# Output product of a hybrid attention layer: attention and hyena halves as three products of rounded parts, and the hyena half two to a step

## The chip, the cores and the metric

The kernel runs on one core of a Trainium2 chip. The metric is device time in microseconds (us) of one execution, as the median of several runs. Engines: PE (TensorE, the matrix engine), DVE (VectorE), ACT (ScalarE), POOL (GpSimd) and SP (SyncE, which issues most DMAs).

## The reference, cut to what matters

One layer over 640 tokens (512 latent, 128 context), five tiles of 128. After a common input projection, attention and a hyena long convolution run side by side. Each half (512 wide) is normalised, and the two are joined by one output projection; then come the second norm with its scale and shift, a router, and 16 experts.

```python
att = attend(q, k, v)
hyo = hyena_mixer(hy, lp)
merged = jnp.concatenate([rms_norm(att, lp['gnorm_att']), rms_norm(hyo, lp['gnorm_hyena'])], axis=-1)
x = x + gt1 * (merged @ lp['w_out'])
h2 = rms_norm(x, lp['norm2_g']) * (1.0 + sc2) + sh2
x = x + gt2 * hier_moe(h2, lp)
```

## The kernel before

All is float32. The input projection and the experts already use a cheaper form: each float32 operand is split into a rounded high part and a low part (the rest), and PE adds high x high, high x low and low x high (`products`). ACT writes high parts (a copy that rounds), DVE low parts (a subtraction). Until this change the output projection, in `mixed`, multiplied plain float32.

The stage in question is a loop over steps v = -1 to 28, written on each engine as its own program; the engines meet only by semaphores. Step v belongs to head pair v: four pairs (`PAIRS`) make one token tile b, so steps 0 to 3 are tile 0, up to steps 16 to 19 for tile 4 (the context tile). Tiles 1 and 2 have four blocks of 128 keys (512 columns of scores per head), tiles 0 and 3 three (384), tile 4 one. In step v the engines do this, in this order:

- PE: scores of pair v+1 (L2089, L2096); the row statistic of a tile (L2129) when v mod 4 is 2; the **fillers** of the table `FILL[v]`; the values product of pair v-1 (L2118); the transposes of the probabilities of pair v (L1877).
- DVE: drains the scores of pair v+1 with bias and minimum (L1437); in step 9 the router's modulated weights (L1499 to L1503), in step 11 its bias (L1516 to L1509); the statistic (L1470); the norm of the probabilities (L1445, L1446); then, when v mod 4 is 1, the sums of squares `out_sums` (L1465, L1466); when v mod 4 is 2, `modulated`, the second norm of a finished tile (L1476 to L1484); then `weighted` for each filler (L1536); when v mod 4 is 0, `out_tile`, the copy of the attention output (L1453) and its multiplication by the norm's gain (L1457).
- ACT: exponentials of pair v+1 (L1072); when v mod 4 is 1, squares of the attention output (L1084) and of the tile before it after both halves are added (`x1_square`, L1089); when v mod 4 is 2, square roots (L1121, L1124), with a table load before and one back; then the copy of the turned probabilities of pair v (L1080).
- POOL: adds the filler of the step before to x (`add_up`, L818), and builds the position bias two pairs ahead (L808).

A filler ("wh", b, n) is the hyena half of the output product of tile b and column half n, ("wa", b, n) the attention half; there are ten of each, of four float32 matmuls 128x512. ("h2", b) transposes a finished tile for the router (L1877, ACT L594, PE L2148). Scores use PSUM banks 0 and 1 in turn, fillers and router transposes banks 5 and 6 in turn; a bank is opened only when its last content is drained.

`w_out` comes in two chunks of 2 MB (column halves), into slots 1 and 2 of a ring. Before the loop, ACT's `hyena_gain` squares the hyena output `hyoT` (L1028) and multiplies it by its gain (L1031).

Of the kernel before, what the change touches and what calls it, by code (L numbers as in the profile page):

```python
# [72 lines left out]
def heads(v):  # L73
# [5 lines left out]
FILL = {2: [("wh", 0, 0)], 3: [("wh", 1, 0)], 4: [("wh", 2, 0)], 5: [("wh", 3, 0)], 6: [("wh", 0, 1)],  # L79
# [4 lines left out]
ROUTE_BEHIND_VALUES = {PAIRS * NT: 2}  # L84
# [182 lines left out]
def program(nc, a, outs):  # L267
    ctx = ExitStack()
    with ctx:
# [22 lines left out]
        yL = [part(f"yL{s}", kb, [P, D]) for s, kb in enumerate((60, 96))]  # L292
        hT = part("hT", 84, [P, KT, TOK], F32)
# [48 lines left out]
        nkb = at(188, CH)  # L342
# [8 lines left out]
        attT = at(186, CB, TOK)  # L351
# [20 lines left out]
        b_buf = [at(176, 512), at(186, 512), at(186, 512)]  # L372
# [107 lines left out]
        att_ok = sem("att_ok")  # L480
# [55 lines left out]
        def win_low(dve, c, r):  # L536
# [4 lines left out]
                              WP[c][r][:, :].bitcast(F32), ALU.subtract).then_inc(wp_low, 1)  # L541

# [213 lines left out]
        def _(pool):  # L756
# [74 lines left out]
            for v in range(-1, STEPS):  # L831
                if v == 1:
                    have(pool, "V", NT - 1)
# [67 lines left out]
        def _(act):  # L901
# [123 lines left out]
            def hyena_gain():  # L1025
# [3 lines left out]
                act.wait_ge(hsq_ok, CB)  # L1029
                for cb in range(CB):  # L1030
                    act.activation(hyoT[:, cb, :], hyoT[:, cb, :], ACT.Copy, scale=chn[:, 1, cb:cb + 1]).then_inc(hg_ok, 1)  # L1031

            for ch, dst, scale in (("q", QT, -DH ** -0.5), ("k", KTt, 1.0)):
# [10 lines left out]
                if ch == "q":  # L1044
# [5 lines left out]
                    load_bias(2)  # L1050
# [3 lines left out]
                    act.dma_start(cv, a["cv"]).then_inc(in_ctx, 16)  # L1054
            for t in range(NT):
                b = full(act, "V", t)
                drain(act.copy(V[:, t, :], b[:, :]), "V", t)
            b = full(act, "nk")
# [16 lines left out]
            def probs_turned(u):  # L1075
# [4 lines left out]
                drain(act.copy(PT[:, u % 2, 0:nk, :].rearrange("p a b -> p (a b)"), b[:, 0:nk * P]), "pt", u)  # L1080

# [17 lines left out]
            for v in range(-1, STEPS):  # L1099
# [4 lines left out]
                if v > PAIRS and v % PAIRS == 1:  # L1104
                    if b < NT:
                        att_squares(b)
# [24 lines left out]
                if 0 <= v < PAIRS * NT:  # L1131
                    for u in heads(v):
                        probs_turned(u)
            for b in (NT - 2, NT - 1):
# [106 lines left out]
        def _(dve):  # L1241
# [177 lines left out]
            for r in range(4):  # L1419
                win_low(dve, 5, r)  # L1420
# [1015 lines left out]
```

## Time and profile before

| | us |
|---|---|
| runs before (three) | 766.28, 766.46, 768.07 |
| median | 766.46 |
| profiled execution: span | 765.7 |
| PE busy | 713.9 (93%) |
| DVE busy | 530.5 (69%) |
| ACT busy | 408.1 (53%) |
| POOL busy | 109.1 (14%) |

The profiled execution is known by its span alone, from the first to the last instruction recorded; its row stands 0.8 us under the median of the three runs. The loop of the steps lies between about 283 and 423 us of the span, the experts fill what follows. PE's busy time counts matmuls that wait inside the engine's pipe, so a PE at 93% is read with the chain of work that ended last: that view says, stretch by stretch, which engine's work the end of the kernel goes back to. A row of it covers several instructions of one line ("x8"); a float32 matmul is recorded as two instructions there, so a filler of four is x8.

### The profile page before, as it was taken

How to read it: one execution, taken by the hardware profiler on the slowest of the kernel's cores; microseconds unless marked ns; L12 is line 12 of the kernel's file. 1: busy time of each engine (PE TensorE's matmuls, PEld its weight loads, DVE VectorE, ACT ScalarE, POOL GpSimd, SP SyncE). 2: the span in 40 equal slices, each digit the busy share in tenths (PEclk: the TensorE clock that was granted, in tenths of full speed). 3: DMA queues.
4: the chain of work that ended last, by engine and by line, in shares of the span. 5: the costliest groups of instructions: out<-in, count | busy, mean ns of one | idle time of the engine just before them, and what ended most of it. 6: DMA issues, size and time to landing. Idle time of an engine off the chain costs nothing.

```text
span 765.7 us, 10729 instructions
## 1 busy us (share of the span) xinstructions
PE 713.9 (93%) x3858; PEld 538.3 (70%) x3858; DVE 530.5 (69%) x831; ACT 408.1 (53%) x617; POOL 109.1 (14%) x164
## 2 busy tenths in 40 slices
PE   5889999989999989999999389999999999999984
PEld 2349998939989755555554277888888888888753
DVE  3355616369442016657556889999999999998897
ACT  2635523330233015445543467888888887788733
POOL 2000000000032006664222100111111111111000
PEclk9999999999999998999999779999999999999998
DMA  9992235023348739900004899999999999999843
GB/s 317 418 390 118 89 132 220 22 89 124 135 103 218 274 135 397 240 1 30 1 28 138 290 349 386 378 370 380 382 373 389 353 397 390 369 385 378 327 197 140
DMA packets 81906, 188.56 MB, mean 246 GB/s; under 512 B 9092, under 2 KB 19492, under 8 KB 78532
## 3 DMA queue, kind: packets, MB, share of 16 engines
q1 hardware_dynamic: 73652, 168.93, 60.1%
q0 software_dynamic: 6448, 16.86, 6.6%
q10 hardware_dynamic: 1760, 2.17, 0.9%
q8 instruction: 27, 0.44, 0.2%
q14 instruction: 19, 0.16, 0.1%
HBM read 175.46 MB, written 18.38 MB: 253 GB/s over the span
## 4 chain that ended last, share of the span: by engine, by line
PE 81%; DVE 7%; DMA 6%; ACT 2%; SPq 2%; issue 1%; ACTq 0%; POOLq 0%; DVEq 0%
PE bank L1967 54%; PE bank L1868 14%; PE bank L1877 6%; DMA slot<-in_w_ada 4%; PE bank L2118 2%; PE bank L1888 2%; DMA slot<-in_w_down 2%; SPq L638 1%; PE bank L2096 1%; PE bank L2089 1%; DVE big L1806 1%; DVE big L1746 1%; DVE big L1816 1%; DVE big L1811 1%; DMA big<-h_scratch,big 1%
## 5 line engine op out<-in xcount | busy, mean ns | idle before, releaser
L1672 DVE TENSOR_TENSOR WL<-slot,WH 128x1024 fp32r<-128x1024 f32 x188 | 219.2, 1220 | 11.7 <-ACT WH L1153 10.6
L1153 ACT CAST WH<-slot 128x1024 fp32r<-128x1024 f32 x188 | 183.5, 1056 | 9.7 <-DMA slot<-in_w_down 4.9
L1967 PE MATMUL bank<-WH,xgTh 128*128 128x512 f32 x256 | 102.3, 400 | 3.0 <-DVE xgTl L1664 3.0
L1967 PE MATMUL bank<-WH,xgTl 128*128 128x512 f32 x256 | 100.7, 393 | 0.0
L1967 PE MATMUL bank<-hTh,WP 128*128 128x384 f32 (+1 forms) x320 | 99.2, 310 | 0.6 <-DVE hTl L1322 0.6
L1967 PE MATMUL bank<-hTh,WL 128*128 128x384 f32 (+1 forms) x320 | 98.7, 308 | 0.0
L1967 PE MATMUL bank<-hTl,WP 128*128 128x384 f32 (+1 forms) x320 | 98.7, 308 | 0.0
L1967 PE MATMUL bank<-WL,xgTh 128*128 128x512 f32 x248 | 96.5, 389 | 0.0
L1868 PE MATMUL bank<-slot,big 128*128 128x512 f32 (+1 forms) x224 | 87.7, 539 | 0.1
L540 DVE TENSOR_TENSOR WL<-slot,WP 128x1024 fp32r<-128x1024 f32 x24 | 29.3, 1237 | 62.1 <-ACT WP L534 61.8
L1877 PE MATMUL bank<-ident,big 128*128 128x128 f32 x424 | 61.4, 285 | 7.6 <-DMA big<-h_scratch,big 4.9
L1868 PEld LDWEIGHTS bank<-slot,big 128*128 128x128 f32 x224 | 40.9, 190 | 35.1 <-issue 33.1
L1967 PEld LDWEIGHTS bank<-hTh,WP 128*128 128x128 f32 x320 | 60.6, 189 | 4.8 <-issue 2.5
L1877 PEld LDWEIGHTS bank<-ident,big 128*128 128x128 f32 x424 | 49.1, 148 | 19.1 <-issue 8.7
L1967 PEld LDWEIGHTS bank<-hTh,WL 128*128 128x128 f32 x320 | 60.6, 189 | 0.0
L1967 PEld LDWEIGHTS bank<-hTl,WP 128*128 128x128 f32 x320 | 60.6, 189 | 0.0
L1967 PEld LDWEIGHTS bank<-WH,xgTh 128*128 128x128 f32 x256 | 48.6, 190 | 12.9 <-DVE xgTl L1664 3.3
L1967 PEld LDWEIGHTS bank<-WH,xgTl 128*128 128x128 f32 x256 | 48.5, 189 | 10.5
L1967 PEld LDWEIGHTS bank<-WL,xgTh 128*128 128x128 f32 x248 | 46.6, 188 | 9.3
L854 POOL DMA_INDIRECT big<-h_scratch,big x16 | 18.5, 1154 | 231.0 <-DVE big L1645 230.7
L1967 PE MATMUL bank<-WH,hidTh 128*128 128x512 f32 x120 | 48.3, 402 | 0.0
L1967 PE MATMUL bank<-WH,hidTl 128*128 128x512 f32 x120 | 46.9, 391 | 0.0
(271 smaller groups left out, 1079.4 us busy)
## 6 DMA issues: line engine op xcount, KB each, us to landing
slot<-in_w_up SPq DMA_DIRECT2D x16, 2048.0 KB, 18.3
slot<-in_w_down SPq DMA_DIRECT2D x16, 2048.0 KB, 18.8
slot<-in_w_gate SPq DMA_DIRECT2D x15, 2048.0 KB, 17.0
slot<-in_w_ada SPq DMA_DIRECT2D x12, 2048.0 KB, 13.0
slot<-in_w_in SPq DMA_DIRECT2D x6, 2048.0 KB, 19.9
y_scratch<-dftp SPq DMA_DIRECT2D x1, 5120.0 KB, 39.9
big<-y_scratch SPq DMA_DIRECT2D x10, 512.0 KB, 8.9
slot<-in_w_out SPq DMA_DIRECT2D x2, 2048.0 KB, 15.3
```

Of the source, the lines that this page charges most:

```text
L540: dve.tensor_tensor(WL[IN_SLOT[i]][:, r, :], slot[IN_SLOT[i]][:, r * QW:(r + 1) * QW], WP[c][r][:, :].bitcast(F32), ALU.subtract).then_inc ...
L638: sp.dma_start(x[:, t, :], a["x"][t * P:(t + 1) * P, :]).then_inc(x_in[t], 16)
L854: pool.indirect_dma_start(out=xg[:, s, :], out_offset=None, in_=h2_dram, in_offset=bass.IndirectOffsetOnAxis(ap=idx[:, s, 0:1].bitcast(U32 ...
L1153: act.copy(WH[:, high_half(w, s), r, :], quarter(n, s, w, r)).then_inc(high_ok[w], 1)
L1672: dve.tensor_tensor(quarter_low(n, s, w, r), quarter(n, s, w, r), WH[:, high_half(w, s), r, :].bitcast(F32), ALU.subtract).then_inc(low_ok ...
L1746: dve.tensor_tensor(yab[:, t, 0], yab[:, t, 0], yab[:, t, 1], ALU.add).then_inc(both_ok, 1)
L1806: dve.tensor_tensor(yab[:, t, 1, half], bank[SUM_BANKS[t][h]][:, :], gt2[:, t // CT, half], ALU.mult).then_inc(f_mul, 1)
L1868: ins = pe.matmul(out, l, r, start=(i == 0), stop=(i == len(terms) - 1))
L1877: return pe.transpose(out, src, ident[:, :])
L1888: ins = pe.matmul(b[rows, :], scond[:, 2 * part + k, :], W[:, k, q * 512:(q + 1) * 512], start=part + k == 0, stop=part == ADA_PARTS - 1 a ...
L1967: ins = pe.matmul(out, l[u], r[v], start=first and i == 0, stop=last and i == 2)
L2118: ins = pe.matmul(bank[4][hp:hp + DH, pair * P:(pair + 1) * P], w, PT[:, u % 2, j, :], start=j == 0, stop=j == len(kts))
```

## The change

1. The output product is made as three products of rounded parts: `mixed` runs 12 matmuls in place of four. The hyena output is split before the loop: ACT's multiplication by the gain now writes its high part `hyoTh` and stands behind the k projection instead of in `hyena_gain`, and DVE writes `hyoTl`.
2. `w_out` is split in four parts (hyena and attention rows of either column half), one at the end of steps 0, 3, 5 and 7 (`SPLIT_AT`): two copies on ACT (`wout_highs`), two subtractions on DVE (`wout_lows`), 128x1024 each. 
3. The attention output of a tile is split when v mod 4 is 1: four copies 128x128 with gain on ACT (`att_highs`), ahead of the squares, and four fused multiply-subtracts on DVE (`att_lows`), ahead of `out_sums`. DVE's multiplication L1457 goes.
4. The hyena fillers stand two to a step in steps 2 to 6; steps 9, 10, 13, 14 and 17 are left without one. The attention fillers keep their steps.
5. The loads of the second norm's scale and shift rows (POOL, four DMAs) move from step 1 to step 7, since the split part of `w_out` lies in their place until then. `load_bias(2)` and the buffer `nkb` move too.

```diff
-FILL = {2: [("wh", 0, 0)], 3: [("wh", 1, 0)], 4: [("wh", 2, 0)], 5: [("wh", 3, 0)], 6: [("wh", 0, 1)],
-        7: [("wa", 0, 0)], 8: [("wa", 0, 1)], 9: [("wh", 1, 1)], 10: [("wh", 2, 1)], 11: [("wa", 1, 0)],
-        12: [("wa", 1, 1), ("h2", 0)], 13: [("wh", 3, 1)], 14: [("wh", 4, 0)], 15: [("wa", 2, 0)],
-        16: [("wa", 2, 1), ("h2", 1)], 17: [("wh", 4, 1)], 19: [("wa", 3, 0)], 20: [("wa", 3, 1)],
+FILL = {2: [("wh", 0, 0), ("wh", 1, 0)], 3: [("wh", 2, 0), ("wh", 3, 0)], 4: [("wh", 4, 0), ("wh", 0, 1)],
+        5: [("wh", 1, 1), ("wh", 2, 1)], 6: [("wh", 3, 1), ("wh", 4, 1)], 7: [("wa", 0, 0)], 8: [("wa", 0, 1)],
+        11: [("wa", 1, 0)], 12: [("wa", 1, 1), ("h2", 0)], 15: [("wa", 2, 0)],
+        16: [("wa", 2, 1), ("h2", 1)], 19: [("wa", 3, 0)], 20: [("wa", 3, 1)],
         21: [("wa", 4, 0)], 22: [("wa", 4, 1)]}
+WOUT_PARTS = [("wh", 0), ("wh", 1), ("wa", 0), ("wa", 1)]
+SPLIT_AT = {0: 0, 3: 1, 5: 2, 7: 3}
+GAINS_STEP = 7
...
             for v in range(-1, STEPS):
-                if v == 1:
-                    have(pool, "V", NT - 1)
+                if v == GAINS_STEP:
+                    full(pool, "wh", NT - 1, 1)
                     pool.wait_ge(m_out[1], 64)
...
+            for cb in range(CB):
+                act.activation(hyoTh[:, cb, :], hyoT[:, cb, :], ACT.Copy, scale=chn[:, 1, cb:cb + 1]).then_inc(hg_ok, 1)
...
+            def wout_highs(i):
+                kind, n = WOUT_PARTS[i]
+                c = CHUNK[("wout", n)]
+                act.wait_ge(chunk_in[IN_SLOT[c]], ARRIVED[c])
+                if kind == "wa":
+                    full(act, "wh", NT - 1, n)
+                for r in range(2):
+                    act.copy(wout_high[kind, n][:, r, :], wout_raw(i, r)).then_inc(wo_high, 1)
+            def att_highs(b):
+                have(act, "o", b)
...
+                for cb in range(CB):
+                    act.activation(attended(b)[0][:, cb, :], oraw[:, b % 2, cb, :], ACT.Copy, scale=chn[:, 2, cb:cb + 1])\
+                       .then_inc(atth_ok, 1)
...
+            def att_lows(b):
+                for cb in range(CB):
+                    dve.wait_ge(atth_ok, b * CB + cb + 1)
+                    high, low = attended(b)
+                    dve.scalar_tensor_tensor(out=low[:, cb, :], in0=oraw[:, b % 2, cb, :], scalar=chn[:, 2, cb:cb + 1],
+                                             in1=high[:, cb, :].bitcast(F32), op0=ALU.mult, op1=ALU.subtract).then_inc(att_ok, 1)
+            def wout_lows(i):
+                for r in range(2):
+                    dve.wait_ge(wo_high, 2 * i + r + 1)
+                    dve.tensor_tensor(wout_low(i, r), wout_raw(i, r), wout_high[WOUT_PARTS[i]][:, r, :].bitcast(F32),
+                                      ALU.subtract).then_inc(wo_low, 1)
...
-                W = chunk(("wout", n)).rearrange("p (k n) -> p k n", n=512)
-                src, k0 = (attT, 0) if kind == "wa" else (hyoT, CB)
-                if kind == "wa":
-                    pe.wait_ge(att_ok, b + 1)
+                i = WOUT_PARTS.index((kind, n))
                 bk = open_bank(*f)
-                close(group(bk[:, :], [(src[:, cb, b * P:(b + 1) * P], W[:, k0 + cb, :]) for cb in range(CB)]))
+                for cb in range(CB):
+                    pe.wait_ge(wo_low, 2 * i + cb // 2 + 1)
+                    if kind == "wa":
+                        pe.wait_ge(att_ok, b * CB + cb + 1)
+                        rows = tuple(v[:, cb, :] for v in attended(b))
+                    else:
+                        rows = tuple(v[:, cb, b * P:(b + 1) * P] for v in (hyoTh, hyoTl))
+                    cols = slice(cb % 2 * 512, cb % 2 * 512 + 512)
+                    ins = products(bk[:, :], rows, (wout_high[kind, n][:, cb // 2, cols], wout_low(i, cb // 2)[:, cols]),
+                                   cb == 0, cb == CB - 1)
+                close(ins)
```

What the change does to the order of instructions is seen at two places. The first is ACT in step 9, from the exponentials of pair 10 (`L1072` before, `L1095` after) to the copies of the turned probabilities of pair 9. Before:

```order
L1072 ACTIVATE big<-big 128x512 x2
L1084 ACTIVATE big<-big 128x512
L1089 ACTIVATE big,ss<-big 128x1024
L1080 COPY big<-bank 128x512 x2
L1072 ACTIVATE big<-big 128x512 x2
```

and with the change:

```order
L1095 ACTIVATE big<-big 128x512 x2
L1125 ACTIVATE attTh<-big,chn 128x128 x4
L1130 ACTIVATE big<-big 128x512
L1135 ACTIVATE big,ss<-big 128x1024
L1103 COPY big<-bank 128x512 x2
```

Four instructions stand new between the exponentials and the square (`L1084`, now `L1130`), and the copies that PE's next values product waits for come behind them all.

The second place is DVE, from the filler drain of step 7 through the scores of pair 9, step 8's first work. Before (a pair of `L1437` rows, a drain with its readout, for each of the two heads):

```order
L1536 SCALAR_TENSOR_TENSOR big<-bank,rsh,big 128x512
L1437 ISA big<-bank,big 128x512
L1437 ISA big 128x1
L1437 ISA big<-bank,big 128x512
L1437 ISA big 128x1
L1445 RECIPROCAL big<-big 128x1
L1446 TENSOR_SCALAR big<-big 128x512
```

and with the change:

```order
L1601 SCALAR_TENSOR_TENSOR big<-bank,rsh,big 128x512
L1522 TENSOR_TENSOR WL<-slot,wa1h 128x1024 x2
L1490 ISA big<-bank,big 128x512
L1490 ISA big 128x1
L1490 ISA big<-bank,big 128x512
L1490 ISA big 128x1
L1498 RECIPROCAL big<-big 128x1
L1499 TENSOR_SCALAR big<-big 128x512
```

The two subtractions of a part of `w_out` stand between the filler's drain and the next scores; DVE takes its instructions in this order.

## Rows read from the trace of the kernel before

**Rows 1.** The page, part 1: busy us, share of the span, instructions

```profile
PE 713.9 (93%) x3858; PEld 538.3 (70%) x3858; DVE 530.5 (69%) x831; ACT 408.1 (53%) x617; POOL 109.1 (14%) x164
```

**Rows 2.** Chain that ended last, 290 to 440 us: start, us, what

```profile
295.02 0.42 PE bank L2089 x4
...
334.43 0.42 PE bank L2089 x4
...
335.50 3.63 PE bank L1868 x8
...
341.17 0.42 PE bank L2089 x4
...
355.38 0.42 PE bank L2089 x4
...
370.90 0.42 PE bank L2089 x4
...
397.10 0.42 PE bank L2089 x4
...
403.58 3.44 PE bank L1868 x8
...
413.98 3.67 PE bank L1868 x8
```

**Rows 3.** The same chain, 215 to 282 us

```profile
251.40 27.35 PE bank L1967 x120
```

**Rows 4.** The page, part 5: costliest groups, busy us, mean ns, idle before

```profile
L1672 DVE TENSOR_TENSOR WL<-slot,WH 128x1024 fp32r<-128x1024 f32 x188 | 219.2, 1220 | 11.7 <-ACT WH L1153 10.6
L1153 ACT CAST WH<-slot 128x1024 fp32r<-128x1024 f32 x188 | 183.5, 1056 | 9.7 <-DMA slot<-in_w_down 4.9
```

**Rows 5.** Groups of ACT by form, 296 to 420 us

```profile
L1072 ACT ACTIVATE big<-big 128x128 f32<-128x128 f32 x8 | 3.1, 394 | 2.0 <-DVE big L1437 2.0
```

**Rows 6.** Line 1031 alone: ns min/median/max, first and last start

```profile
L1031 ACT ACTIVATE big<-big,chn x4: 816/816/834, 223.0 to 225.2; 128x640 f32<-128x640 f32 x4
```

**Rows 7.** Groups of DVE by form, 200 to 280 us

```profile
L1407 DVE SCALAR_TENSOR_TENSOR big<-big,chn,bank 128x128 f32<-128x128 f32 x4 | 1.1, 341 | 0.3 <-PE bank L1868 0.3
```

**Rows 8.** Timeline of all engines, 275 to 297 us: start, us, what

```profile
291.23 0.83 ACT L1080 COPY big<-bank 128x384 f32<-128x384 f32 x2
...
292.25 0.56 DVE L1437 CUSTOM_DVE_ANT_0 big<-bank,big 128x384 f32<-128x384 f32 x1 [0.28 <-PE bank L2096]
...
294.82 2.13 POOL L793 DMA_DIRECT2D big<-m_scratch  x4 [3.90 <-DMA m_scratch<-big]
```

**Rows 9.** Tile slot, 275 to 300 us: its two w_out loads, issued 278.8 and 280.7

```profile
DMA to landing us min/median/max: 8.1/15.3/22.5
```

**Rows 10.** Timeline of ACT, 333 to 373 us

```profile
340.77 1.07 ACT L1080 COPY big<-bank 128x512 f32<-128x512 f32 x2 [2.99 <-PE bank L1877]
...
344.43 0.61 ACT L1084 ACTIVATE big<-big 128x512 f32<-128x512 f32 x1
...
345.90 0.18 ACT L1089 ACTIVATION_READ_ACCUMULATOR big<-big 128x1 f32 x1
...
350.25 0.72 ACT L1072 ACTIVATE big<-big 128x512 f32<-128x512 f32 x1 [1.16 <-DVE big L1437]
```

**Rows 11.** Timeline of DVE, 333 to 373 us

```profile
353.59 0.16 DVE L1566 RECIPROCAL rsh<-ss 128x1 f32<-128x1 f32 x1 [1.11 <-ACT ss L1124]
...
360.99 0.75 DVE L1536 SCALAR_TENSOR_TENSOR big<-bank,rsh,big 128x512 f32<-128x512 f32 x1
362.81 0.56 DVE L1437 CUSTOM_DVE_ANT_0 big<-bank,big 128x384 f32<-128x384 f32 x1 [1.07 <-PE bank L2096]
...
366.44 0.75 DVE L1536 SCALAR_TENSOR_TENSOR big<-bank,rsh,big 128x512 f32<-128x512 f32 x1 [0.96 <-PE bank L1868]
```

**Rows 12.** Windows of 2 us: busy us of engines, PEclk, DMA share, GB/s

```profile
284.00:286.00 2.00, 0.51 (x5) 0.10 (x1) 0.00 (x0) 0.17 (x1) 0.00 (x0) 1.00 1.07 401
...
288.00:290.00 2.00, 1.77 (x9) 1.05 (x6) 1.75 (x7) 0.75 (x4) 0.76 (x2) 0.50 1.01 387
```

More of the change, by code:

```diff
@@ L292, in program @@
         yL = [part(f"yL{s}", kb, [P, D]) for s, kb in enumerate((60, 96))]
+        hyoTh, hyoTl = part("hyoTh", 186, [P, CB, TOK]), part("hyoTl", 104, [P, CB, TOK])
+        attTh, attTl = ([part(f"attT{x}{i}", kb + d, [P, CB, P]) for i, kb in enumerate((12, 186, 190))]
+                        for x, d in (("h", 0), ("l", 2)))
+        wout_high = {(kind, n): part(f"{kind}{n}h", kb, [P, 2, QW])
+                     for (kind, n), kb in zip(WOUT_PARTS, (84, 92, 24, 40))}
         hT = part("hT", 84, [P, KT, TOK], F32)
@@ L541, in win_low, with wout_raw, wout_low, attended @@
                               WP[c][r][:, :].bitcast(F32), ALU.subtract).then_inc(wp_low, 1)
+        def wout_raw(i, r):
+            kind, n = WOUT_PARTS[i]
+            return slot[IN_SLOT[CHUNK[("wout", n)]]][:, (r + 2 * (kind == "wh")) * QW:(r + 1 + 2 * (kind == "wh")) * QW]
+        def wout_low(i, r):
+            kind, n = WOUT_PARTS[i]
+            return WL[IN_SLOT[CHUNK[("wout", n)]]][:, r + 2 * (kind == "wh"), :]
+        def attended(b):
+            i = 0 if b == 0 else 2 - b % 2
+            return attTh[i], attTl[i]
         def expert_steps(eng, p, step):
@@ L1028, in hyena_gain @@
                     act.activation(sq[:, cb, :], hyoT[:, cb, :], ACT.Square).then_inc(hsq_ok, 1)
-                act.wait_ge(hsq_ok, CB)
-                for cb in range(CB):
-                    act.activation(hyoT[:, cb, :], hyoT[:, cb, :], ACT.Copy, scale=chn[:, 1, cb:cb + 1]).then_inc(hg_ok, 1)
             for ch, dst, scale in (("q", QT, -DH ** -0.5), ("k", KTt, 1.0)):
@@ L1080, in probs_turned @@
                 drain(act.copy(PT[:, u % 2, 0:nk, :].rearrange("p a b -> p (a b)"), b[:, 0:nk * P]), "pt", u)
+            def wout_highs(i):
+                kind, n = WOUT_PARTS[i]
+                c = CHUNK[("wout", n)]
[6 more added lines that the diff above has]
+                have(act, "o", b)
+                if b == 0:
+                    act.wait_ge(kv_out, 32)
+                elif b < 3:
+                    full(act, "wh", NT - 1, 1)
+                else:
+                    full(act, "wa", b - 2, 1)
+                for cb in range(CB):
+                    act.activation(attended(b)[0][:, cb, :], oraw[:, b % 2, cb, :], ACT.Copy, scale=chn[:, 2, cb:cb + 1])\
+                       .then_inc(atth_ok, 1)
             def att_squares(b):
@@ L1420, in _ @@
                 win_low(dve, 5, r)
+            for cb in range(CB):
+                dve.wait_ge(hg_ok, cb + 1)
+                dve.scalar_tensor_tensor(out=hyoTl[:, cb, :], in0=hyoT[:, cb, :], scalar=chn[:, 1, cb:cb + 1],
+                                         in1=hyoTh[:, cb, :].bitcast(F32), op0=ALU.mult, op1=ALU.subtract).then_inc(hyl_ok, 1)
             b = full(dve, "hst")
```

28 lines of the change are left out of this document (17 added, 11 removed).

## The prediction

> **What bounds the kernel now.** I read the engines' busy shares first: PE 93%, DVE 69%, ACT 53% [rows 1]. Then the chain that ended last [rows 2]: from 295 to 418 us it is PE almost alone, step behind step. Step 8 is the pattern: it starts at 334.43 with the scores, its filler runs from 335.50 for 3.63 us, values and transposes fill the rest to 341.17. Of 6.74 us the filler is 3.63; the other 3.11 (1.07 scores, 1.02 values, 1.02 transposes) remain in any step of tiles 1 and 2 (2.7 to 2.9 with three blocks, 1.2 with one). Next come ACT's and DVE's timelines [rows 10, 11]: what they do within a step ends before PE asks for it, because the filler covers it. So two questions decide: what a filler costs in the new form, and what is left in the steps that lose theirs.
>
> **The filler in the new form.** The V projection is made of just such triples, 128x512: 120 matmuls in 27.35 us [rows 3], 0.228 each. Twelve make 2.73 us against 3.63, or 3.44 where the weight load hides [rows 2]. The 19 fillers up to the end of step 21 take about 68.3 us now (14 of 3.63, the rest down to 3.44 [rows 2]) and 51.9 then: **16.4 us of PE work less**. The twentieth (step 22) lies beside DVE's final chain and I give it nothing. That is the whole gain; all else is what comes back.
>
> **The start, 1.3 us.** ACT ends the copies of step 0 at 292.06 [rows 8]; two high copies of 1.06 [rows 4] follow to 294.2, and DVE's two lows of 1.22 [rows 4] end at about 295.5. Behind them waits the drain of pair 2's scores, now at 292.25 [rows 8]. PE wants banks 0 and 1 back at 295.02 [rows 2] and gets them at 296.1 and 296.5. The chunk isn't late: the first landed 8.1 us after its issue, at 286.9, the second 22.5 us after, at 303.2 [rows 9], and its split is due only at about 313. The moved loads cost nothing: four issues took POOL 2.13 us [rows 8], and at step 7 the bias queued behind them (for pair 9) is due over 9 us later, while POOL has some 8 us to do; without that cover it would be the 2.13.
>
> **Steps 2 to 7.** Two fillers a step make 8.6 us of PE; ACT and DVE have room, and the splits at the ends of steps 3 and 5 delay DVE's scores by 3 to 4 us, which their consumers (a whole step later) don't see. No loss. Their x adds (POOL) also fit.
>
> **Step 8, 1.9 us.** The split at the end of step 7 is used at once. ACT's two copies end 0.67 after PE's transposes (in step 8, 340.77 plus 1.07 [rows 10], against 341.17 [rows 2]); then 1.06 for the high and 1.22 for the low [rows 4]: 2.95 us after step 7, while PE has 1.07 of scores to do. It waits 1.9.
>
> **Steps 9 and 10, 2.3 us.** The attention split is priced by two rows: the same operation at 128x640 took ACT 0.82 [rows 6], an activation of 128x128 took 0.39, starts 0.30 apart [rows 5]. By size I take the second: four cost 1.3. (Bounds: 0.9 to 3.3, the last four times 0.82.) DVE's four lows at 0.34 or less [rows 7] run beside ACT's and end just after. In step 9, exponentials end 3.26 us after PE begins (341.17 to 344.43 [rows 2, 10]); then 1.3 of highs, 1.65 of both squares (344.43 to 346.08 [rows 10]) and 1.07 of copies. PE's values product of step 10 waits for those, then come 1.02 and 1.02: 9.3 us for both steps. Now they take 14.21 with two fillers (341.17 to 355.38), 7.04 without. Lost 2.3; only 1.3 of it is new work, the rest was always there, under the fillers.
>
> **Steps 11 and 12, 2.1 us.** Here DVE is the chain. From the exponentials of step 10 (350.25 [rows 10]) to the root's reciprocal 3.34; to the filler drain of step 11 at 360.99, 7.40 (with the second norm); then step 12's scores and norms 2.6 (362.81 to 365.4), all [rows 11]. Thus 13.3 us after those exponentials, which start 2.0 before step 11, comes the drain that frees a bank for the router transposes: 11.3 into the pair of steps. From it to step 13 took 4.46 (366.44 to 370.90 [rows 2, 11]). That is 15.8 against 15.52 now, where two cheaper fillers should have made it 13.7.
>
> **Steps 13 to 16, 3.6 us; 17 and 18, 3.0 us; 19 to 21, 0.9 us.** By the same sums. 13 and 14: 2.65 for scores and exponentials, 1.3, 1.65, 0.86, then 0.81 twice, 8.1; 15 and 16: 12.7 by DVE's chain of norm and drains; 20.8 together against 26.20 now [rows 2] less two fillers and two savings (17.2). 17 and 18: 1.6, 1.3, 1.65, 0.5, then 0.37 twice, 5.8, against 6.48 less 3.63. Steps 19 to 21 begin late for DVE, whose norm from step 18 holds the drains, and the last attention filler follows ACT's new copies.
>
> **Sum.** 16.4 less 1.3, 1.9, 2.3, 2.1, 3.6, 3.0 and 0.9 (15.1) is 1.3 us. The filler of step 21 would start near 411 instead of 413.98 [rows 2] and end some 1.3 earlier; from there DVE's chain, the routing and the experts follow unchanged. Against the profiled span of 765.7 that gives 764.4; the median of the runs is 0.8 higher, so 765.1. Rounding in the handoffs is a microsecond either way. Splitting the hyena output before the loop costs nothing: its four copies move behind the k projection, where ACT then has 27 us of V projection [rows 3] nearly free, and DVE's four lows too; if it were exposed it would be 3.3.
>
> **A clock that may fall.** The granted clock was 1.00 while PE was busy 0.51 of 2 us, and 0.50 afterwards, when it had work again [rows 12]; it stayed at 1.2 GHz for about 7 us. In the new steps 17 and 18 PE would have some 0.7 us of work in 3.5 us (from its transposes of pair 17 to the values of step 18), and in 13 and 14 about 1.1 of 3.8. The Trainium skill (TensorE: Matmul & The Clock Gate, What's actually happening) says that the throttled state is the default and activity releases it. By that rule these gaps would bring 1.2 GHz back, and the cheaper fillers behind them would lose most of what they won. No row shows a gap of this kind within the loop, so I keep it as a rival.
>
> **The rivals.** 0.3% (2.3 us) is about what a measurement of this kernel can tell from no change.
>
> *A: as summed.* 765.1, own range 761 to 767: handoffs and the price of the copies. For it: each term is a queue order and a row. Chance 0.48, a third of it under 764.2.
>
> *B: the clock falls in a gap (13/14 or 17/18).* For it: rows 12's pattern. Against: the fall there followed a gap with an entirely idle stretch. Half speed for up to 7 us on a PE that is partly waiting costs 1.5 to 4: 766.6 to 769. Chance 0.18.
>
> *C: ACT's and DVE's tails bind less.* I let every wait in steps 9 to 18 stand in full. If the light steps' backlog is half as long (shorter copies of 0.9 us a tile, drains that slip ahead), half of 11.9 us comes back: 759, and at the extreme, with only the start and step 8 lost, 753. Against: DVE's queue is strict and its 13.3 us are measured. Chance 0.20.
>
> *D: slower.* The high copies cost what the row of the same operation says, 0.82 each: four are 3.3 instead of 1.3, on the path in steps 9, 13 and 17 and partly in 21: 2.0 three times and 0.9, 6.9 us, so 765.1 plus 6.9, 772. It decides from about 0.6 us a copy, where 3.6 more cancels the gain and the 2.3. For it: the only row with exactly that operation. Against: its size is five times as large, and 128x128 took 0.39. Chance 0.09.
>
> *E: nothing for the product*, since 12 matmuls wait on parts one by one: then PE keeps 3.63 a filler and the sum is plus 10 or more. Against: rows 3 waits on its parts in the same way. Chance 0.05.
>
> **The numbers.** Predicted 765.1. The range must leave out no more than 2 in 10: 758.5 (under half of C, 0.08, below it) to 770.0 (most of D and E, 0.12, above). Faster by over 0.3%: a third of A (0.16), all C (0.20), 0.36. Slower: D, E (0.14) and a little of B (0.04), 0.18. Same: 0.46.
>
> **What the new profile would show.** Fillers of twelve in 2.73 us; scores' drains after the lows in step 0, PE idle about 1.3 us at 295; PE waiting for DVE's low near 1.9 us in step 8; the values product of steps 10, 14 and 18 released by ACT's copy (L1080 before) and the statistic L2129 by DVE's sums; PE idle rising by some 15 us between 295 and 418, and ACT's highs 0.30 apart. I am wrong if that idle time is under 8 us, if the granted clock leaves 1.00 within the loop, or if ACT's 128x128 copy is over 0.5.

## The result: slower by 0.7%, through a clock that fell three times

| | before | with the change |
|---|---|---|
| median, us | 767.09 (6 runs, 764.08 to 768.29) | 771.17 (6 runs, 770.34 to 774.27) |
| ratio | | 1.0068, interval 1.0045 to 1.0090 |
| predicted | | 765.1, range 758.5 to 770.0 |
| span of the profiled execution | 765.7 | 768.8 |
| mean granted clock over the runs | 0.972 to 0.981 (21 runs of before beside the first experiments) | 0.966 to 0.970 (6 runs) |

The change is slower by 4 us in the medians and by 5 in the ratio, where 1.3 us less was forecast, and the result lies outside the range. The page of the changed kernel, part 1 and the row of the granted clock in 40 slices, against [rows 1]:

```profile
PE 707.4 (92%) x3938; PEld 558.9 (73%) x3938; DVE 544.1 (71%) x858; ACT 420.2 (55%) x645; POOL 112.5 (15%) x164
...
PEclk9999999999999998999988879999999999999998
```

and the clock row of the kernel before:

```profile
PEclk9999999999999998999999779999999999999998
```

PE's busy time fell by 6.5 us only, though the fillers save about twice that. A slice is 19.2 us: the 21st and 22nd, 384 to 423 us, hold 8 and 8 where the kernel before has 9 and 9 (the two behind them are the routing, slow in both). The chain that ended last says where, against [rows 2]:

```profile
297.58 5.69 PE bank L2035 x24
...
346.71 1.95 issue
348.66 3.01 PE bank L2035 x12
...
360.49 0.55 PE bank L2197 x2
361.04 1.90 PE bank L2186 x16
...
388.70 4.14 PE bank L2035 x12
...
407.85 4.60 PE bank L2035 x12
...
413.19 2.77 PE bank L2035 x12
...
419.38 3.00 PE bank L2035 x12
```

L2035 is the new filler, L2186 the values product, L2197 the row statistic, L2157 the first of the scores. A single filler takes 2.94 to 3.01 us, a pair up to 5.69; but the fillers of steps 15 and 19 take 4.14 and 4.60, and the values product of step 10 takes 1.90 instead of 1.02. The windows of 2 us at two of these places have the reason in their third column from the right, PEclk:

```profile
358.00:360.00 2.00, 0.39 (x4) 0.00 (x0) 2.00 (x6) 2.00 (x5) 0.75 (x2) 1.00 0.03 7
360.00:362.00 2.00, 1.51 (x12) 1.52 (x14) 1.76 (x8) 1.76 (x5) 0.96 (x3) 0.63 0.06 7
362.00:364.00 2.00, 2.00 (x16) 1.67 (x13) 1.16 (x4) 1.97 (x4) 0.91 (x2) 0.52 0.03 8
...
404.00:406.00 2.00, 0.00 (x0) 0.00 (x0) 1.82 (x8) 2.00 (x6) 0.00 (x0) 0.72 0.98 360
406.00:408.00 2.00, 1.98 (x9) 1.62 (x10) 1.35 (x9) 1.98 (x8) 0.00 (x0) 0.50 1.04 397
```

PE is busy 0.39 and 0.00 of 2 us, and then, full of work, runs at a granted clock of 0.52 and 0.50, the second being 1.2 GHz throughout. The same happens at 384. PE's timeline has the idle stretch ahead of each fall in square brackets, and the starts of scores and thus of steps (353.65 is step 9, 364.39 step 11, 378.57 step 13, 387.90 step 15, 401.61 step 17):

```profile
283.17 0.48 PE L2157 MATMUL bank<-ckT,big 64*128 64x128 f32 x2
...
353.65 0.49 PE L2157 MATMUL bank<-ckT,big 64*128 64x128 f32 x4
...
360.49 0.55 PE L2197 MATMUL bank<-ones,big 128*128 128x1 f32 x2 [2.10 <-DVE big L1531]
...
364.39 0.49 PE L2157 MATMUL bank<-ckT,big 64*128 64x128 f32 x4
...
378.57 0.49 PE L2157 MATMUL bank<-ckT,big 64*128 64x128 f32 x4
...
384.11 0.38 PE L2197 MATMUL bank<-ones,big 128*128 128x1 f32 x2 [1.93 <-DVE big L1589]
...
387.90 0.80 PE L2157 MATMUL bank<-big 64*128 64x128 f32 x4
...
401.61 0.49 PE L2157 MATMUL bank<-big 64*128 64x128 f32 x4
...
406.02 0.59 PE L2197 MATMUL bank<-ones,big 128*128 128x1 f32 x2 [2.39 <-DVE big L1589]
```

The kernel before had fillers in steps 10, 13, 14 and 17, and its granted clock stayed at 1.00 from 295 to 418. The profile is no accident of one execution: the mean granted clock of each run of the changed kernel lies under that of every run of before. A microsecond at half clock lowers the mean by 0.5/768; the average over the runs is 0.968 against 0.977, and 0.009 less is 14 us more at 1.2 GHz. The windows of the profiled execution show 17 (3.4, 6.8 and 6.8).

**One measure for all that follows.** The time before the loop differs from one execution to the next by up to 3 us, so I compare the stage alone, in the profiled executions: from the first scores of the loop (pair 0, step -1; the expectation of e13_behind calls them pair 1) to the end of step 21's filler. In the kernel before this row begins it, and [rows 2] ends it (413.98 plus 3.67):

```profile
282.84 0.48 PE L2089 MATMUL bank<-ckT,big 64*128 64x128 f32 x2
```

That is 134.81 us. In the changed kernel it is 283.17 to 422.38, 139.21. The forecast for it was 134.8 less 1.3, 133.5.

### The profile page after: what moved, and what is told of

It is laid out like the page before. It is cut to its first block, busy times and chain, and to the rows that moved or that the text cites. A ratio compares the mean times of both kernels' runs of the same rounds, so it can differ in the third digit from the quotient of the medians.

```text
span 768.8 us, 10980 instructions
## 1 busy us (share of the span) xinstructions
PE 707.4 (92%) x3938; PEld 558.9 (73%) x3938; DVE 544.1 (71%) x858; ACT 420.2 (55%) x645; POOL 112.5 (15%) x164
## 4 chain that ended last, share of the span: by engine, by line
PE 78%; DVE 8%; DMA 6%; ACT 3%; issue 2%; SPq 2%; ACTq 0%; POOLq 0%; DVEq 0%
PE bank L2035 61%; PE bank L1945 5%; PE bank L1936 5%; DMA slot<-in_w_ada 4%; PE bank L1956 2%; PE bank L2186 2%; DMA slot<-in_w_down 2%; SPq L661 1%; PE bank L2157 1%; PE bank L2164 1%; DVE big L1874 1%; DVE big L1814 1%; DVE big L1884 1%; DVE big L1879 1%; DMA big<-h_scratch,big 1%
## 5 line engine op out<-in xcount | busy, mean ns | idle before, releaser
L2035 PE MATMUL bank<-WH,xgTh 128*128 128x512 f32 x256 | 102.2, 399 | 3.0 <-DVE xgTl L1732 3.0
L2035 PE MATMUL bank<-WH,xgTl 128*128 128x512 f32 x256 | 100.6, 393 | 0.0
L2035 PE MATMUL bank<-hTh,WP 128*128 128x384 f32 (+1 forms) x320 | 99.2, 310 | 0.6 <-DVE hTl L1371 0.6
L2035 PE MATMUL bank<-hTl,WP 128*128 128x384 f32 (+1 forms) x320 | 98.7, 308 | 0.0
L2035 PE MATMUL bank<-hTh,WL 128*128 128x384 f32 (+1 forms) x320 | 98.7, 308 | 0.0
L2035 PE MATMUL bank<-WL,xgTh 128*128 128x512 f32 x248 | 96.5, 389 | 0.0
L1945 PE MATMUL bank<-ident,big 128*128 128x128 f32 x424 | 63.0, 290 | 8.2 <-DMA big<-h_scratch,big 4.9
L2035 PEld LDWEIGHTS bank<-hTh,WP 128*128 128x128 f32 x320 | 60.6, 189 | 4.8 <-issue 2.5
L2035 PEld LDWEIGHTS bank<-hTl,WP 128*128 128x128 f32 x320 | 60.6, 189 | 0.0
L2035 PEld LDWEIGHTS bank<-hTh,WL 128*128 128x128 f32 x320 | 60.6, 189 | 0.0
L2035 PEld LDWEIGHTS bank<-WH,xgTh 128*128 128x128 f32 x256 | 48.6, 190 | 12.9 <-DVE xgTl L1732 3.3
L2035 PEld LDWEIGHTS bank<-WH,xgTl 128*128 128x128 f32 x256 | 48.5, 189 | 10.5
L2035 PEld LDWEIGHTS bank<-WL,xgTh 128*128 128x128 f32 x248 | 46.6, 188 | 9.3
L831 POOL TENSOR_TENSOR big<-maskb,big 128x128 f32<-128x128 f32 x80 | 40.1, 532 | 75.0 <-DVE big L1490 58.4
L2035 PE MATMUL bank<-WH,hidTh 128*128 128x512 f32 x120 | 48.3, 402 | 0.0
L2035 PE MATMUL bank<-WH,hidTl 128*128 128x512 f32 x120 | 46.9, 391 | 0.0
L2035 PE MATMUL bank<-WL,hidTh 128*128 128x512 f32 x120 | 46.7, 389 | 0.0
## 6 DMA issues: line engine op xcount, KB each, us to landing
slot<-in_w_ada SPq DMA_DIRECT2D x12, 2048.0 KB, 13.3
```

The lines of the kernel that those rows point to most:

```text
L831: last = pool.tensor_tensor(out, in0, in1, ALU.subtract)
L1945: return pe.transpose(out, src, ident[:, :])
L2035: ins = pe.matmul(out, l[u], r[v], start=first and i == 0, stop=last and i == 2)
```

## The experiments

Theory F: the falls of the clock are the loss; the waits themselves are about what was forecast. Its rival W: the waits on ACT and DVE are the loss, and a slow PE beside them is incidental. P: the three products save nothing. Ratios are against runs of the kernel before on the same chip; "stage" is the measure above; "from step 7" runs from the scores of step 7 to the same end (it can be compared only among kernels with the same work behind step 7: e2_place with e5_place_warm, all others of the changed kernel's family among themselves); "falls" are counted from step 7 on.

| kernel | median, us | ratio, interval | stage, us | from step 7, us | falls |
|---|---|---|---|---|---|
| before |  | 1 | 134.81 |  | 0 |
| changed | 771.17 | 1.0068 (1.0045 to 1.0090) | 139.21 | 82.87 | 3 |
| e1_warm | 766.00 | 0.9992 (0.9978 to 1.0007) | 134.63 | 78.21 | 1 |
| e2_place | 773.18 | 1.0092 (1.0071 to 1.0114) | 140.33 | 78.24 | 1 |
| e3_split6 | 770.64 | 1.0056 (1.0034 to 1.0078) | 136.77 | 80.24 | 3, shorter |
| e5_place_warm | 771.58 | 1.0068 (1.0048 to 1.0088) | 139.71 | 77.63 | 0 |
| e9_r5 | 772.58 | 1.0088 (1.0065 to 1.0110) | 139.48 | 82.41 | 4 |
| e6_warm8 | 765.90 | 0.9990 (0.9974 to 1.0006) | 136.23 | 76.84 | 0, one at 296 |
| e11_x | 770.00 | 1.0044 (1.0026 to 1.0062) | 139.36 | 80.10 | 3, one at 293 |
| e8_w8_r5_x | 766.29 | 1.0006 (0.9986 to 1.0025) | 133.64 | 76.75 | 0 |
| e13_behind | 768.91 | 1.0026 (1.0009 to 1.0042) | 138.11 | 81.09 | 3 |
| e14_behind_d8 | 768.00 | 1.0015 (0.9999 to 1.0030) | 136.13 | 79.28 | 2 |
| e15_dose1 | 766.58 | 0.9999 (0.9982 to 1.0017) | 137.67 | 79.77 | 2, one at 296 |
| e17_all | 767.39 | 1.0015 (0.9995 to 1.0034) | 134.45 | 77.53 | 0 |

The stage holds one thing that no edit of the loop's later steps can reach. Every execution, the kernel before included, has a fall in steps -1 to 1 (somewhere between 283 and 296 us), and those of e6_warm8, e11_x and e15_dose1 have a second one at 293 to 303. Their stages are 1 to 3 us longer by it, which is why the column from step 7 stands beside.

### The clock alone: e1_warm

```diff
+                if v in (10, 14, 18):
+                    idle_bank = open_bank(*FILL[v + 1][0])
+                    for i in range(2):
+                        pe.matmul(idle_bank[:, :], ident[:, :], V[:, CT, :], start=True, stop=True)
                 if stat_of(v) is not None:
                     att_stat(stat_of(v))
```

> The changed kernel with two extra float32 matmuls 128x512 on PE (identity times a tile of V, into the idle filler bank, read by nobody) in steps 10, 14 and 18, ahead of the row statistic, where PE of the changed kernel sat idle for 2.1, 1.9 and 2.4 us. They are 1.7 us of PE work each time and change no result. Theory F (the falls of the granted clock are the loss): the clock stays at 1.00 from 295 to 430 us, the values, transposes and fillers behind the three gaps take their full-speed time again, and 5 to 6.5 us come back, so 765 to 766 against 767 before and 771 for the changed kernel. Rival W (the waits on ACT and DVE are the loss, and a slow PE only fills time in which it would wait): the clock stays up but less than 1.5 us come back, 769.5 to 771. Rival P (the three products save nothing): as W.

Nothing is taken away; two matmuls whose result nobody reads are added in each of three steps, where PE would wait. Its timeline, with L2262 the added ones, then its windows, then its chain:

```profile
281.24 0.48 PE L2157 MATMUL bank<-ckT,big 64*128 64x128 f32 x2
...
353.35 0.49 PE L2157 MATMUL bank<-ckT,big 64*128 64x128 f32 x4
...
358.03 1.98 PE L2262 MATMUL bank<-big,ident 128*128 128x512 f32 x4
...
362.56 0.49 PE L2157 MATMUL bank<-ckT,big 64*128 64x128 f32 x4
...
377.34 0.49 PE L2157 MATMUL bank<-ckT,big 64*128 64x128 f32 x4
...
385.33 0.49 PE L2157 MATMUL bank<-big 64*128 64x128 f32 x4
...
397.57 0.49 PE L2157 MATMUL bank<-big 64*128 64x128 f32 x4
```

```profile
358.00:360.00 2.00, 2.00 (x7) 0.73 (x5) 1.97 (x8) 2.00 (x5) 0.00 (x0) 1.00 0.05 8
360.00:362.00 2.00, 1.83 (x23) 1.57 (x23) 1.76 (x7) 1.98 (x5) 1.48 (x4) 1.00 0.05 6
```

```profile
344.86 1.96 issue
346.81 4.56 PE bank L2035 x12
...
403.20 2.75 PE bank L2035 x12
...
412.88 2.99 PE bank L2035 x12
```

The clock stays at 1.00 where it had been 0.63 and 0.52, the filler of step 19 takes 2.75 instead of 4.60, and the ratio goes from 1.0068 to 0.9992: more work, and the loss is gone. F's 765 to 766 is met, P is out: the filler costs 3.0 and not 3.6. One fall is new, behind the wait of step 8 (346.81, a filler of 4.56), where the changed kernel's execution had the same wait of 1.95 and no fall.

Two more comparisons need no new kernel. The changed kernel, e1_warm, e15_dose1 and e6_warm8 differ in their dummies alone; at 1.2 GHz they spend 17.1, 3.4, 6.8 and 0 us from step 7 on (by the PEclk column of their windows), and take 82.87, 78.21, 79.77 and 76.84 us from there: 0.35 to 0.43 us more for each at the low clock. And the runs of one kernel differ in the same way: e9_r5's two at a mean granted clock of 0.961 and 0.964 took 775.81 and 775.00 us, its four at 0.968 to 0.970 took 771.60 to 772.69.

### The places alone: e2_place and e5_place_warm

e2_place is the kernel before with the new table `FILL` and nothing else of the change; e5_place_warm has the dummy matmuls in addition.

> The kernel before with one edit, the new table of fillers (hyena two to a step in steps 2 to 6, none in steps 9, 10, 13, 14, 17); the products stay plain float32, nothing is split. It isolates the placement. Theory F and rival W both: PE's work is the same as before, the light steps wait for ACT and DVE (1 us in 9 and 10, some 2 each in 11 to 12, 13 to 16 and 17 to 18, less than in the changed kernel, since no copies of the attention split stand there), 6 to 8 us; by F the clock falls as well, 3 to 5 us more: 776 to 780 by F, 773 to 775 by W with the clock at 1.00 or without effect. Rival P: the placement costs 0 to 2 us, 767 to 769.

> The kernel of the new placement with plain float32 products (the kernel before with the new table of fillers) and the two extra matmuls in steps 10, 14 and 18. By F the clock stays at 1.00 and 3 to 5 us come back against the same without them, 772 to 775; what is left over the kernel before is the price of the waits alone. By W the two are within 1.5 us. By P both are within 2 us of the kernel before.

The chain of e2_place at one double filler (first row), then its timeline at three light steps (L2129 is its statistic, L2118 its values product):

```profile
303.29 7.06 PE bank L1868 x16
```

```profile
361.52 0.35 PE L2129 MATMUL bank<-ones,big 128*128 128x1 f32 x2 [0.84 <-DVE big L1466]
...
384.70 0.88 PE L2118 MATMUL bank<-big 128*64 128x128 f32 x12 [0.45 <-ACT big L1080]
...
403.69 0.38 PE L2129 MATMUL bank<-ones,big 128*128 128x1 f32 x2 [1.67 <-DVE big L1524]
```

The same matmuls in the new places cost 5.5 us of stage, with a single short fall (at 405), behind which a filler takes 5.13 in place of 3.44. The waits that the fillers had hidden cost the rest, without any split of anything. The time, 773.18, is W's 773 to 775 and not F's 776 to 780: F had assumed three falls here, and the stretches of steps 10 and 14, 0.84 and 0.76 us, had none. The dummies bring e5_place_warm to a clock of 1.00 from step 2 on but only 0.6 us less stage, and a time of 771.58, under F's 772 to 775 with less won than F asked for: there was one fall to remove, and two dummies (1.98 us) are longer than the waits, so that they lie on PE's path. So placement alone is a loss of 0.9%, a part of which the cheaper filler wins back.

### The wait of step 8: e3_split6 and e6_warm8

```diff
-SPLIT_AT = {0: 0, 3: 1, 5: 2, 7: 3}
+SPLIT_AT = {0: 0, 3: 1, 5: 2, 6: 3}
```

> The changed kernel with the last part of w_out split at the end of step 6 instead of 7. The trace of the changed kernel shows PE idle 1.95 us in step 8 for DVE's low part. All theories: that wait goes. F: the whole stage comes 1.9 us earlier but the three falls of the clock stay, 1 to 2 us less than the changed kernel, 769 to 770; where the gaps fall against the clock's own rhythm may shift by one fall, 2 us either way. W: 1.9 less, 769. If nothing changes, the DVE chain behind it (scores of pair 9 on) did not depend on that wait.

From its chain at step 8:

```profile
344.24 1.47 DVE WL L1522
345.71 1.23 DVE big L1490 x4
```

Splitting the last part of `w_out` a step earlier only moves the wait: now the scores' drain (L1490) stands behind the low part (L1522) on DVE. The ratio falls by 0.0012, inside the intervals. Three falls remain, at 360, 384 and 404, each some 3 us long and not up to 7. The stage's 2.4 us come from there and not from step 8: steps 13 to 16 are 1.5 shorter than in the changed kernel, steps 17 to 21 0.9, while step 9 begins only 0.3 earlier.

e6_warm8 is e1_warm with two dummies in step 8, in place of that wait.

> e1_warm (two unused float32 matmuls of 128x512 at the start of steps 10, 14 and 18) with two more such matmuls in step 8, ahead of the filler that waits 1.96 us for the low part of w_out. They take about that wait. Theory F: the fall that was left in e1_warm (a filler of 4.56 us in place of 3.0) goes too, so no low clock between 295 and 418 us: 1.5 us less than e1_warm, 764.4. Theories W and P: nothing is won, 766, since the wait stays.

The fall behind step 8 is gone, as F said, and from step 7 on the 1.4 us are won in the profiled execution (76.84 against 78.21). But the time doesn't show them: 765.9 against 766.0. The profile has a fall at 296 to 303 instead, behind a wait of 1.78 us at the loop's start, before any dummy. In the changed kernel's execution PE was still at half clock there and idled 0.70 only; in e8_w8_r5_x it idled 2.00 at the same place without a fall. The mean granted clock over the 12 runs of each is 0.975 in e1_warm and 0.976 in e6_warm8 (3.4 us less at the low clock would be 0.002 more), so on the average little low clock was removed. By the medians F has no point here.

### Shorter waits without dummies: e9_r5, e11_x

e9_r5 sets `ROUTER_STEP` to 5. e11_x moves `x1_square(b - 1)` behind the loop of `probs_turned` on ACT.

> The changed kernel with the router's modulated weights and bias made in steps 5 and 7 instead of 9 and 11 (ROUTER_STEP = 5): DVE has 1.05 us less between the scores and the norms of step 9, and 1.7 us less in step 11. No dummy matmuls. Theory F (the clock falls are most of the loss): PE's wait for the statistic in step 10 shrinks from 2.10 to about 1.1 us, the fall behind it goes away or comes later, the two falls at 383 and 404 stay; 1.1 plus 1.4: about 768.7 against the changed kernel's 771.2, with two falls in the loop in place of three. Theory W (ACT's and DVE's waits are the loss and the clock is incidental): up to 2.7 us of DVE work leave the chain, 768.5, with the number of falls having nothing to do with it. Theory P (the three products save nothing): 770 to 771.

> The changed kernel with one edit: ACT squares the finished tile before (x1_square, 1.04 us) behind the copies of the turned probabilities, not ahead of them, in steps 9, 13 and 17. ACT's sum of work is the same, but the copies come 1.04 us earlier and PE's idle stretches of steps 14 and 18 shorten from 1.9 and 2.4 to about 0.9 and 1.4 us; the stretch of step 10 ends with DVE's statistic and stays. Theory F: the falls at 383 and 404 go, 5.2 us, and something of the waits: 765 to 766. Theory W: the wait only moves from ACT's copies to the next exponentials and DVE's norm chain: 769.5 to 771. P: 770 to 771.

F's forecast misses in both (768.7 and 765 to 766); e11_x is in W's 769.5 to 771, e9_r5 is slower than any theory had it. Rows of the timeline, of e9_r5 and then of e11_x:

```profile
359.93 0.35 PE L2197 MATMUL bank<-ones,big 128*128 128x1 f32 x2 [1.94 <-DVE big L1531]
360.89 1.44 PE L2186 MATMUL bank<-big 128*64 128x128 f32 x16 [0.60 <-ACT big L1103]
```

```profile
384.33 0.38 PE L2197 MATMUL bank<-ones,big 128*128 128x1 f32 x2 [1.93 <-DVE big L1589]
...
404.45 0.38 PE L2197 MATMUL bank<-ones,big 128*128 128x1 f32 x2 [2.39 <-DVE big L1589]
```

I had misread who is waited for. On PE the statistic stands ahead of the values product, and the statistic needs DVE's sums, these ACT's square, and this the four high parts. In e9_r5 the statistic comes 0.56 us earlier (359.93 against 360.49), not the 1.05 taken from DVE, and PE is at it 0.40 earlier too, because the router's small products left PE's step 9 together with DVE's work: step 10's stretch shrinks by 0.16 only (2.10 to 1.94). Behind it the values product now waits 0.60 for ACT's copies, which it didn't in the changed kernel. Moving `x1_square`, which stands behind the square, does nothing to the stretches of steps 14 and 18 (1.93 and 2.39 as before); what it removes is a second wait in step 14, the 0.46 us in which the changed kernel's values product waits for the copies. With the long stretches unchanged the falls stayed, three in e11_x's loop and four in e9_r5, behind step 8 as well. e11_x's 2.8 us less from step 7 on are mostly its falls: 3.4 us each where two of the changed kernel's were 6.8, as in e3_split6 (80.10 and 80.24 us). Why e9_r5's median is 1.4 us above the changed kernel's, with less DVE work in the light steps, is not settled; the two intervals overlap, and there are six runs of each.

### All of it together: e8_w8_r5_x

> All of it together: the changed kernel with the dummy matmuls in steps 8, 10, 14 and 18, the router's weights in steps 5 and 7, and x1_square behind the copies. Theory F with the waits as the rest of the loss: no fall, and up to 2 us less of waits in steps 9 to 18 than e6_warm8: 762 to 763.5, faster than the kernel before. If the dummies now exceed the shortened waits (1.9 us against some 1 us), they lie on PE's path and it stays at 764 to 765. P: not under 766.

Both ends of the stage, from its timeline and its chain:

```profile
282.52 0.48 PE L2157 MATMUL bank<-ckT,big 64*128 64x128 f32 x2
```

```profile
413.19 2.97 PE bank L2035 x12
```

No fall, and a stage of 133.64 us, the shortest of all and 1.2 us under before. The median doesn't show it (766.29, 1.0006, interval 0.9986 to 1.0025): 1.2 us is half of what a measurement of this kernel can tell. Both numbers that F had given, 762 to 763.5 and 764 to 765, were missed. From step 7 on it takes 76.75 us, against 76.84 with the dummies alone (e6_warm8): once the clock stays up, the two moved pieces of work are worth nothing that these two executions show.

### Real work in another order: e13_behind, e14_behind_d8, e17_all, and half the dose: e15_dose1

```diff
@@ ACT, steps 9, 13, 17
-                    att_highs(b)
-                    att_squares(b)
-                    x1_square(b - 1)
                     for u in heads(v):
                         probs_turned(u)
+                    att_highs(b)
+                    att_squares(b)
+                    x1_square(b - 1)
@@ PE, steps 10, 14, 18
-                att_stat(stat_of(v))
                 values(v - 1)
                 for u in heads(v):
                     turn_probs(u)
+                att_stat(stat_of(v))
```

The diff is shortened; `ROUTER_STEP` is 5 here too.

> No dummy matmuls; the order of real work is changed so that PE's idle stretches of steps 10, 14 and 18 come apart. In steps 9, 13 and 17 ACT does the copies of the turned probabilities first, then the high parts and both squares; in steps 10, 14 and 18 PE asks for the statistic behind the values and the transposes, not ahead of them; the router's weights are made in steps 5 and 7. Theory F: the values no longer wait, the statistic waits 0.3 to 1.2 us instead of 1.9 to 2.4, and the falls at 360, 384 and 405 go (6.5 us) with some 3 us of waits: 762 to 764, the stage from the scores of pair 1 to the end of the filler of step 21 at 131 to 134 us instead of 139.2. Theory W: the late statistic now delays DVE's norms of the next pair, so the wait moves to the fillers of steps 11, 15 and 19: 768 to 770. If the falls come whatever the length of a stretch: 767 to 769, with falls near 361, 384 and 405.

> The kernel of e13_behind with the two dummy matmuls ahead of the filler of step 8 alone, where PE waits about 1.95 us for the low part of w_out. Theory F: equal to e13_behind where that one shows no fall behind step 8, and 1.5 to 2 us less where it does: 761 to 763, the shortest stage of all. Theory W: as e13_behind.

> e1_warm with one dummy matmul in place of two in steps 10, 14 and 18: PE works 0.95 us and idles 1.0 to 1.4 us ahead of the statistic, where it idled 1.9 to 2.4 us before. The waits end when they did, so only the clock can change. Theory F with idle stretches as the trigger: no falls there, 766 as e1_warm. If a stretch of about 1 us is enough to trigger them: three falls, 770 to 771. Theory W: 770 to 771.

e13_behind's timeline at steps 14 and 18, and its chain at step 15's filler (its lines are numbered anew, as in e17_all: L2203 is the statistic, L2041 the filler, L2163 the scores and L1496 their drain):

```profile
385.00 0.38 PE L2203 MATMUL bank<-ones,big 128*128 128x1 f32 x2 [0.95 <-DVE big L1595]
...
404.42 0.58 PE L2203 MATMUL bank<-ones,big 128*128 128x1 f32 x2 [1.82 <-DVE big L1595]
```

```profile
386.46 4.47 PE bank L2041 x12
```

The idle stretches shrink to 0.46, 0.95 and 1.82, and the fall of step 10 is gone; those of steps 14 and 18 are not, although 0.95 us is half of what stood there. In e15_dose1 stretches of 0.83 and 0.88 us in steps 10 and 14 went without a fall, and 1.33 in step 18 had one. So F's "stretches of about 2 us" was too simple. In time, 768.9 is not F's 762 to 764 but within W's 768 to 770, and equally within the 767 to 769 of falls that come at any length. e14_behind_d8 has no fall behind step 8 any more and 1.8 us less from step 7 on; its 768.0 against 768.9 is inside the intervals and again not F's 761 to 763. e15_dose1 is 766.58, as F said: half the dummies give back nearly all that two did, since the waits end when they did and only the clock differs.

e17_all puts dummies ahead of the late statistic, one in step 14 and two in step 18.

> The kernel of e14_behind_d8 (reordered copies and statistic, dummies in step 8) with dummy matmuls in the stretches in which its clock still fell: one ahead of the late statistic in step 14 (it idled 0.95 us there) and two in step 18 (1.82 us). Theory F: both falls go, 1.4 and 1.7 us or more of slow fillers with them, so the stage shrinks from 136.1 to about 132.5 us and the time to 763.5 to 765, below the kernel before. Theory W: nothing but the clock is touched, so the time stays at 768.

No fall is left, and the stage is 134.45 instead of the 132.5 that F asked for; the time is 767.39 (1.0015). This is W's part: with the clock at 1.00 the reordered kernel is no faster than the plain one with dummies (77.53 us from step 7 on against e6_warm8's 76.84). Steps 10 and 14 are 1.2 us shorter each than there, steps 11 and 15 longer by 1.1 and 1.5. Its timeline shows PE waiting for the drain of scores at the end of step 15, where e6_warm8's doesn't wait:

```profile
391.04 0.69 PE L2163 MATMUL bank<-big 64*128 64x128 f32 x4 [0.89 <-DVE big L1496]
```

That the late statistic and norm hold DVE up is the likely reason, not a tested one. PE's wait of 1.16 us ahead of the second transposes for the router in step 12 is not it: e1_warm has 1.13 there.

No version tried is measurably faster than the kernel before. The open rival is to keep hyena fillers in the light steps in the new form. It wasn't tried: the high parts of `w_out`'s attention rows, the gains of the second norm and the attention parts lie in memory that the hyena parts hold until step 7. So no run shows whether the three products pay with the old places.

## Why the prediction was wrong

**The step that failed is "A clock that may fall".** It named the gaps in 13/14 and 17/18 and the pattern in [rows 12], and then kept it as rival B, one fall of 1.5 to 4 us with a chance of 0.18, because no row showed such a gap within the loop. One did: [rows 12] are steps -1 and 0 of this very loop, where PE of the kernel before idled 2.54 us ahead of the scores at 287.04 and then ran at 0.50. For the new light steps the prediction's own sum put 2.3 us of waits in steps 9 and 10, 3.6 in 13 to 16 and 3.0 in 17 and 18; it should have asked of each what the clock does there. The price of a fall was about right, the count wasn't: three came, and with them 6 us. Step by step, from the rows of timeline and chain above (starts of steps; the forecast for 19 to 21 is the old 14.07 less three savings of 0.71, 0.71 and 0.94, plus 0.9; 17 and 18 end with the start of step 19's filler, 19 to 21 with the end of step 21's; chain rows of 17's start are 401.68 and 397.64):

| steps | predicted | e1_warm | changed | difference |
|---|---|---|---|---|
| 9 and 10 | 9.3 | 9.21 | 10.74 | 1.5 |
| 11 and 12 | 15.8 | 14.78 | 14.18 | -0.6 |
| 13 to 16 | 20.8 | 20.23 | 23.04 | 2.8 |
| 17 and 18 | 5.8 | 5.56 | 6.17 | 0.6 |
| 19 to 21 | 12.6 | 12.67 | 14.53 | 1.9 |

The last column adds to 6.2 us, in three falls (1.5, of which 0.6 comes back in steps 11 and 12, where e1_warm waits longer for DVE; 2.8; 2.5, which spans steps 17 to 21). e1_warm's stage is only 4.6 us shorter since it has a fall of its own of 1.6 us in step 8 (4.56 against 3.0). The forecast of 765.1 plus 6.2 is 771.3, and measured were 771.17; that this closes so well is in part luck, as the filler and the waits were both wrong and hid each other (below).

The Trainium skill (TensorE: Matmul & The Clock Gate, What's actually happening) says that the throttled state is the default and that activity releases it. The trace agrees, by the dummies: with 1.98 us of useless work at 358 the clock stayed at 1.00, without it, it was 0.52 from 362 to 364. The prediction drew the right consequence from it and set its weight too low.

**The filler in the new form** was mis-sized: 2.94 to 3.01 alone, 2.8 in a pair and 2.75 to 2.77 in the context tile, not 2.73 everywhere. The 19 take 54.7 at full clock (28.3 for ten in pairs, 26.4 for nine), so 13.6 us were saved, not 16.4. The row it was priced by [rows 3] is one run of 120; the old filler's price [rows 2] is a short row that has the cost of a start in it. Twelve at 0.228 make 2.73, and 0.1 to 0.3 comes once with each run of fillers behind other work (5.57 to 5.69 for the 24 of a pair, 2.94 to 3.01 for 12 alone), though not in the context tile. It doesn't come with each sum of twelve: in step 2 the second filler's first matmul starts 0.23 us after the last of the first does, like any other.

**The waits** were oversized by about as much, which hid that error. Without falls from step 7 on the stage would be e1_warm's 134.63 less 1.6, 133.0: 134.8 less 13.6 is 121.2, so the waits are 11.8, not 15.1. One microsecond of the difference is in steps 11 and 12, where I let DVE's 13.3 us stand in full. Right were the start (the low parts of step 0 end at 294.53 in the changed kernel's chain, 295.5 was forecast, and the scores of step 2 start 13.02 us into the stage against 12.11 before, 0.9 later where 1.3 was), step 8 (1.95 against 1.9), and steps 9 and 10 (9.21 against 9.3).

**The high parts** cost what the smaller row said. Groups of the changed kernel by form, against [rows 5]:

```profile
L1125 ACT ACTIVATE attTh<-big,chn 128x128 fp32r<-128x128 f32 x20 | 6.3, 388 | 0.0
...
L1515 DVE SCALAR_TENSOR_TENSOR attTl<-big,chn,attTh 128x128 fp32r<-128x128 f32 x20 | 6.1, 364 | 0.0
```

0.39 each: rival D (0.82 each, 772) gave nearly the right time by a mechanism that wasn't there. C was wrong on the whole, though some waits bound less. E is out by the filler's 3.0.

**Which wait ends last in the light steps** was right in part: the prediction let ACT's copies release the values product in all three steps, and DVE's sums the statistic ahead of it. In steps 10 and 18 of the changed kernel it is the statistic, in the order squares, sums, statistic (in 14 and 18 with the router's logits, L1589, one short instruction behind the sums). In step 14 it is ACT's copies, as summed, and its chain shows it:

```profile
384.17 0.74 ACT big L1103 x2
...
384.95 1.55 PE bank L2186 x12
```

e11_x was built on the copies ending the long stretches of steps 14 and 18, which the statistic ends, and e9_r5 on DVE alone in step 10; so both moved little.

## What to carry to other kernels

A filler that looks like the bound can also be what keeps the clock up: when a change takes PE work out of a step and your own sum puts a wait there, count those waits, and charge each with the half clock behind it, not one for the kernel. A cheap test is to put useless matmuls into the wait; if the time falls, the clock was the loss. And price a short run from a short run: a row of 120 matmuls hides the start that a run of 12 pays.

## What was unexpected of the hardware

No length of an idle stretch decides alone. In steps 8, 10, 14 and 18 of the changed kernel and the experiments, stretches of 1.67 to 2.39 us were followed by 1.2 GHz in 19 of 21 cases; the two without were the 1.95 us of step 8 in the changed kernel and in e11_x, while 1.91 to 1.96 us at the same place had a fall in e1_warm, e9_r5, e13_behind and e15_dose1. One of 1.33 us (e15_dose1, step 18) had a fall. Of the shorter ones (0.46 to 0.95 us) two had one (0.95 both times, in step 14, with a light step ahead), all others none. At the loop's start, ahead of the scores of step 2, stretches of 1.71, 1.78 and 1.95 us had a fall and one of 2.00 (e8_w8_r5_x) had none. The Trainium skill (TensorE: Matmul & The Clock Gate, What's actually happening) says that the window in which activity is judged runs freely and is not reset when a kernel starts. That the same wait falls in one execution and not in the next agrees with this, but no run here shows the window itself.

The low state lasted between 3 and 7 us in these loops, with PE at work for all or most of it, so that a wait of 2 us cost up to another 2.8 us behind it.
